# Two blocks of a transformer on one core: the memory's projections moved ahead of the mixing's output projection, one weight buffer for several stages, and attention maps started a chunk earlier

## The reference, cut to what matters

```python
for l in range(2):
    x = x + 0.5 * swiglu_ffn(rms_norm(x, ffn1_norm_g[l]), ...)        # ffn1
    proj = rms_norm(x, mix_norm_g[l]) @ w_mix_in[l]                   # mix_in
    y_rwkv = rwkv7_time_mix(...)      # 8 heads of 64; its end: y -> (y - mean) / sqrt(var + eps) * ln_g + ln_b + bonus, * g
    y_moba = moba_attention(...)
    x = x + concatenate([y_rwkv, y_moba]) @ w_mix_out[l]              # mix_out
    # memory_cross_attention, with 4 heads of 256:
    q    = rms_norm(x, xattn_norm_g[l]) @ w_q                         # xattn_q
    k, v = split(rms_norm(mem, mem_norm_g[l]) @ w_kv)                 # xattn_kv; mem: 256 x 1024
    x = x + (softmax(q @ k.T / 16) @ v) @ w_o                         # xattn_o
    x = x + 0.5 * swiglu_ffn(rms_norm(x, ffn2_norm_g[l]), ...)        # ffn2
# second block: proj = h @ w_in; mLSTM heads hm (4 x 128); differential attention hd (4 x 128)
merged = sigmoid(g_m) * (hm @ w_br_m) + sigmoid(g_d) * (hd @ w_br_d)
x = x + gate1 * (merged @ w_out)
x = x + gate2 * hierarchical_moe(...)
```

## Time and profile before

| | before |
|---|---|
| median of 3 runs | 2149.92 us (2147.03 to 2153.95) |
| the profiled execution: its time, its span | 2156.08 us, 2154.3 us |
| mean granted clock of TensorE | 0.963 |
| PE busy | 2025.2 us (94% of the span) |
| DVE busy | 1451.4 us (67%) |
| ACT busy | 1075.4 us (50%) |
| POOL busy | 328.7 us (15%) |
| moved by DMA | 401.93 MB, mean 187 GB/s |

### The profile page before, as it was taken

How to read it: one execution, slowest core, us unless ns; L and a number is a source line. 1 busy time by engine, 2 the same in 40 slices (tenths; PEclk the granted TensorE clock), 3 DMA queues, 4 the chain that set the end, 5 groups by cost and what they waited for, 6 DMA issues and landing times. The chain is left out here.

```text
span 2154.3 us, 34205 instructions
## 1 busy us (share of the span) xinstructions
PE 2025.2 (94%) x14008; PEld 1766.3 (82%) x14008; DVE 1451.4 (67%) x1876; ACT 1075.4 (50%) x1625; POOL 328.7 (15%) x182
## 2 busy tenths in 40 slices
PE   6999998699999989999987999998999889999999
PEld 5887887599888868879886997887899887888887
DVE  5774664475577467747637656764776557999997
ACT  5443662244544354437523445443655435777775
POOL 1650004000056006400040002630000000000000
PEclk9999999899999999999998999999999988999999
DMA  9653420054456456534203435653433324999995
GB/s 378 244 202 131 173 102 2 22 195 157 176 217 232 176 195 234 214 137 159 77 3 119 176 115 202 252 213 118 141 133 118 118 105 172 363 375 373 369 369 205
DMA packets 56854, 401.93 MB, mean 187 GB/s; under 512 B 6280, under 2 KB 7456, under 8 KB 8448
## 3 DMA queue, kind: packets, MB, share of 16 engines
q1 hardware_dynamic: 52320, 370.05, 46.1%
q0 software_dynamic: 4384, 29.74, 3.8%
HBM read 398.70 MB, written 1.06 MB: 186 GB/s over the span
## 5 line engine op out<-in xcount | busy, mean ns | idle before, releaser
L315 DVE TENSOR_TENSOR weights_lo<-ring,weights_hi 128x1024 fp32r<-128x1024 f32 x696 | 929.5, 1379 | 156.7 <-ACT weights_hi L305 155.8
L305 ACT CAST weights_hi<-ring 128x1024 fp32r<-128x1024 f32 x696 | 693.9, 1049 | 256.0 <-PE ps L329 255.7
L327 PE MATMUL ps<-weights_hi,act_hi 128*128 128x512 f32 (+1 forms) x832 | 320.3, 385 | 27.8 <-DVE weights_lo L315 23.3
L327 PE MATMUL ps<-act_hi,weights_hi 128*128 128x256 f32 x992 | 296.0, 298 | 26.4 <-DVE weights_lo L315 16.4
L329 PE MATMUL ps<-weights_hi,act_lo 128*128 128x512 f32 (+1 forms) x832 | 314.8, 378 | 0.0
L328 PE MATMUL ps<-weights_lo,act_hi 128*128 128x512 f32 (+1 forms) x832 | 313.8, 377 | 0.0
L328 PE MATMUL ps<-act_lo,weights_hi 128*128 128x256 f32 x992 | 288.1, 290 | 0.0
L329 PE MATMUL ps<-act_hi,weights_lo 128*128 128x256 f32 x992 | 287.6, 290 | 0.0
L327 PEld LDWEIGHTS ps<-act_hi,weights_hi 128*128 128x128 f32 x992 | 197.7, 199 | 34.6 <-DVE weights_lo L315 18.2
L327 PEld LDWEIGHTS ps<-weights_hi,act_hi 128*128 128x128 f32 x832 | 159.2, 191 | 57.6 <-DVE weights_lo L315 23.5
L328 PEld LDWEIGHTS ps<-act_lo,weights_hi 128*128 128x128 f32 x992 | 197.9, 200 | 0.1
(11 more groups left out here) (538 smaller groups left out, 3303.4 us busy)
## 6 DMA issues: line engine op xcount, KB each, us to landing
ring<-stream SPq DMA_DIRECT2D x348, 1024.0 KB, 4.9
stretch<-ada_in POOLq DMA_DIRECT2D x12, 1024.0 KB, 5.2
modulation_rows<-ada_in POOLq DMA_DIRECT2D x12, 1024.0 KB, 5.4
h<-mem_in POOLq DMA_DIRECT2D x2, 1024.0 KB, 5.3
consts<-w_consts SPq DMA_DIRECT2D x1, 1376.0 KB, 7.9
x<-x_in SPq DMA_DIRECT2D x1, 1024.0 KB, 4.9
stretch<-mem_in POOLq DMA_DIRECT2D x1, 1024.0 KB, 9.9
bias_slid<-bias_scratch SPq DMA_DIRECT2D x1, 1024.0 KB
```

The costliest lines, as they stand in the source:

```text
L305: core.nc.scalar.copy(self.hi[:, self.place(i), part], core.slot(chunk)[:, part]).then_inc(self.rounded.sem, 1)
L315: core.nc.vector.tensor_tensor(self.lo[:, self.place(i), part], core.slot(chunk)[:, part], self.hi[:, self.place(i), part].bitcast(F32), A ...
L327: nc.tensor.matmul(out, lhs[0], rhs[0], start=start, stop=False, **kw)
```

## The change

**In memory_stage** the stream's order is keys (chunks 0 to 3), values (4 to 7), mix_out (8 to 11), queries, output. The first products need no `y`: its centring, variance, norm, transposes and gating move out of `rwkv_stage` and stand between the products of chunks 0 to 4. Memory is normalized on POOL inside `rwkv_stage`, by four products of 128x1024. ACT copies keys and values. Chunk 0 is handed over by halves (`await_half`). x's norm before the queries becomes a `LateNorm` with its `add` and `total` at chunk 12; 1/rms enters as the scale of the scores. Buffers move to make room: `rwkv_g` lies in `b.decay`, `q`, `v`, `probs` in `b.stretch`.

**Splitters.** One runs from layer 0's xattn_kv over ffn2, layer 1's ffn1 and mix_in; ffn2 of layer 0 rounds two chunks further, and layer 1's ffn1 takes them with split=2.

**second_stage.** FIRST_TICK is 8, so that map 11's transposes and values fall within the chunk loop; the head norm of the attention stands earlier in the tail, each of its steps ahead of a branch product or of a chunk's split.

```diff
-        plan += [(("ffn1", layer), 3 * FFN_STEPS), (("mix_in", layer), 13), (("mix_out", layer), 4),
-                 (("xattn_kv", layer), 8), (("xattn_q", layer), 4), (("xattn_o", layer), 4),
+        plan += [(("ffn1", layer), 3 * FFN_STEPS), (("mix_in", layer), 13), (("xattn_kv", layer), 8),
+                 (("mix_out", layer), 4), (("xattn_q", layer), 4), (("xattn_o", layer), 4),
                  (("ffn2", layer), 3 * FFN_STEPS)]
...
-            for t in range(TT):
-                dve.wait_ge(y_done.sem, y_done.at(t + 1))
-                V(nc.vector.reduce_sum(stat[:, 0, 8 * t:8 * t + 8], bank8(t), AX))
-            V(nc.vector.tensor_scalar(stat[:, 0, :], stat[:, 0, :], 1.0 / 64, None, ALU.mult))
-            for t in range(TT):
-                V(tt(yt[:, t], bank8(t), stat[:, 0, 8 * t:8 * t + 8].unsqueeze(2).to_broadcast([P, 8, 64]), ALU.subtract))
-            V(tt(yq, yt, yt, ALU.mult))
...
-            nc.gpsimd.dma_start(h[:, :, :], b.mem_in).then_inc(b.mem_loaded.sem, 16)
+            nc.gpsimd.dma_start(h[:, :, :], b.mem_in).then_inc(mem_loaded.sem, 16)
+            pool.wait_ge(mem_loaded.sem, mem_loaded.at(16))
+            gain = core.param("mem_norm_g", layer)
+            for i in range(2):
+                part = h[:, 4 * i:4 * i + 4, :]
+                tt(part, part, b.mem_rs[:, :].unsqueeze(1).to_broadcast([P, 4, S]), ALU.mult).then_inc(mem_scaled.sem, 1)
+                pool.wait_ge(mem_scaled.sem, mem_scaled.at(i + 1))
+                tt(part, part, gain[:, 4 * i:4 * i + 4].unsqueeze(2).to_broadcast([P, 4, S]),
+                   ALU.mult).then_inc(b.mem_normed.sem, 1)
...
-            from_state(3, St[:, 1], 3).then_inc(y_done.sem, 1)
-            for t in range(TT):
-                pe.wait_ge(normed.sem, normed.at(t + 1))
...
+            from_state(3, St[:, 1], 3)
...
-                weights.await_split(pe, c)
+                if c:
+                    weights.await_split(pe, c)
                 if c >= banks:
                     sig, k = taken(c - banks)
                     pe.wait_ge(sig.sem, sig.at(k))
+                elif c >= 2:
+                    pe.wait_ge(centred.sem, centred.at(c - 1))
                 w = weights.parts(c, "p (k n) -> p k n", k=KB)
...
-                if c == 5:
-                    pe.wait_ge(added.sem, added.at(1))
-                    nc.tensor.matmul(ps[:, TURN, 0:S], core.const("ones"), rs[:, :], start=True,
-                                     stop=True).then_inc(summed.sem, 1)
-                elif c == values + 1:
+                if c == 3:
+                    for t in range(TT):
+                        pe.wait_ge(y_normed.sem, y_normed.at(t + 1))
+                        for i in range(4):
+                            ins = nc.tensor.transpose(ps[:, 4 + i, t * P:(t + 1) * P],
+                                                      yq[:, t, 2 * i:2 * i + 2, :].rearrange("p e n -> p (e n)"),
+                                                      core.const("ident"))
+                            if t == TT - 1:
+                                ins.then_inc(y_turned.sem, 1)
+                elif c == outs:
+                    acts.total(pe, TURN)
+                elif c == outs + 1:
...
+            weights.round_half(act, 0, 0)
+            round_mem(range(4))
+            weights.round_half(act, 0, 1)
+            round_mem(range(4, KB))
             weights.round(act, 1)
             weights.round(act, 2)
+            for t in range(TT):
+                act.wait_ge(centred.sem, centred.at(t + 1))
+                ins = nc.scalar.activation(yq[:, t], yt[:, t], ACT.Square)
+            ins.then_inc(y_squared.sem, 1)
             for c in range(queries):
+                if c < values:
                     act.wait_ge(core.used, start + c + 1)
                     nc.scalar.copy(place(c), bank(c)).then_inc(by_scalar.sem, 1)
+                elif c < outs:
+                    j = c - values
+                    act.wait_ge(by_vector.sem, by_vector.at(j + 1))
+                    acts.round(act, range(2 * j, 2 * j + 2))
+                    if j == 0:
+                        act.wait_ge(y_ready.sem, y_ready.at(KB))
+                    ins = nc.scalar.activation(y[:, 2 * j:2 * j + 2, :], x[:, 2 * j:2 * j + 2, :], ACT.Square)
+                    if c == outs - 1:
+                        ins.then_inc(acts.squared.sem, 1)
...
+            weights.subtract_half(dve, 0, 0)
+            split_mem(range(4))
+            weights.subtract_half(dve, 0, 1)
+            split_mem(range(4, KB))
             weights.subtract(dve, 1)
+            centre_y()
             weights.subtract(dve, 2)
...
             for c in range(queries):
...
-                if c < outs:
+                if values <= c < outs:
+                    j = c - values
                     dve.wait_ge(core.used, start + c + 1)
-                    dst = x[:, 2 * c:2 * c + 2, :]
+                    dst = x[:, 2 * j:2 * j + 2, :]
                     nc.vector.tensor_tensor(dst, dst, bank(c), ALU.add).then_inc(by_vector.sem, 1)
-                elif taken(c)[0] is by_vector:
+                    acts.subtract(dve, range(2 * j, 2 * j + 2))
+                elif c >= outs:
                     dve.wait_ge(core.used, start + c + 1)
                     nc.vector.tensor_copy(place(c), bank(c)).then_inc(by_vector.sem, 1)
+                if c == outs + 1:
+                    acts.invert(dve)
+                    V(nc.vector.tensor_scalar(row_scale[:, 0, :], rs[:, :], float(S) ** -0.5, None, ALU.mult))
+                    V(nc.vector.tensor_scalar(row_scale[:, 1, :], rs[:, :], -float(S) ** -0.5, None, ALU.mult))
                     front(0)
...
+                if c == 0:
+                    vary_y()
+                elif c == 1:
+                    norm_y()
                 if c + 1 < queries:
                     weights.subtract(dve, c + ways)
-                if c < 2:
-                    split_mem(range(4 * c, 4 * c + 4))
-                elif c == 4:
-                    dve.wait_ge(squared.sem, squared.at(1))
-                    nc.vector.reduce_sum(rs[:, :], h[:, :, :].rearrange("p k t -> p t k"), AX).then_inc(added.sem, 1)
+                if c == 4:
+                    gate_y()
+                elif c == 5:
+                    split_y(range(4))
                 elif c == 6:
+                    split_y(range(4, KB))
+                elif c == outs:
+                    acts.add(dve)
...
-    MAPS, M_MAPS, FIRST_TICK = 12, 4, 9
+    MAPS, M_MAPS, FIRST_TICK = 12, 4, 8
...
             branch_unit(BR_M, 0)
-            do_values(MAPS - 1)
-            branch_unit(BR_M, 1)
             pe.wait_ge(head_normed.sem, head_normed.at(4))
             head_sums(1, squares_d)
+            branch_unit(BR_M, 1)
+            head_turns(1)
             branch_unit(BR_M + 1, 0)
-            head_turns(1)
+            head_spreads(1)
             branch_unit(BR_M + 1, 1)
-            head_spreads(1)
             for c in range(BR_D, OUT):
                 branch_unit(c, 0)
...
             merge_m(0)
+            invert_heads(1)
             merge_m(1)
             weights.subtract(dve, BR_M + ways)
-            invert_heads(1)
             merge_m(2)
-            merge_m(3)
-            weights.subtract(dve, BR_M + 1 + ways)
             dve.wait_ge(head_spread.sem, head_spread.at(2))
             for j in range(4):
                 nc.vector.scalar_tensor_tensor(heads_d[:, j, :], heads_d[:, j, :], b.subln[:, 0:1],
                                                ps[:, E0 + j // 2, j % 2 * S:(j % 2 + 1) * S], ALU.mult,
                                                ALU.mult).then_inc(head_normed.sem, 1)
             split_y(1)
+            merge_m(3)
+            weights.subtract(dve, BR_M + 1 + ways)
             merge_d(0)
             merge_d(1)
             weights.subtract(dve, BR_D + ways)
...
-            move_turned(MAPS - 1)
-            take_values(MAPS - 1)
-            weights.round(act, BR_M + ways)
             root_heads(1)
             move_heads(1)
+            weights.round(act, BR_M + ways)
+            round_y(1)
             weights.round(act, BR_M + 1 + ways)
-            round_y(1)
             weights.round(act, BR_D + ways)
             round_merged(0)
...
+            run = ExitStack()
+            weights = Splitter(core, run, STREAM_AT["ffn1", 0][0], 3 * FFN_STEPS + 13)
             for layer in range(DEPTH):
...
-                        weights = Splitter(core, run, STREAM_AT["ffn1", layer][0], 3 * FFN_STEPS + 13)
...
-                    weights = Splitter(core, run, STREAM_AT["mix_out", layer][0], 20 + 3 * FFN_STEPS)
...
+                more = layer + 1 < DEPTH
+                ffn_stage(core, ("ffn1", layer), FFN_STEPS, weights, x, h, core.param("ffn1_norm_g", layer), h,
+                          modulation=(b, ada_in, y, 12 * layer, 6), loads=() if layer else loads[3:], split=2 if layer else 0,
+                          further=1, stretch=b.stretch)
```

(40 more changed lines are left out.)

224 lines of the change are left out of this document (99 added, 125 removed).

## The result

The changed kernel takes 2133.53 us (median of 4 runs, 2131.79 to 2137.32); before, the median over all runs beside it is 2151.7 us. The ratio over these runs is 0.9928, with a 95% interval of 0.9906 to 0.9949: 15.5 us faster by the ratio, between 11 and 20 us; the two medians alone are 18.2 us apart. The prediction was 2132, with 2118 to 2142 as its range.

A forecast was written before the change was run, and what follows sets the result against it. PE, busy 94% of the span, was taken as the bound, so its products plus its waits. Terms of 5.3 (layer 0), 5.0 (layer 1), 3.9 (Splitter) and 3.7 (second_stage) gave 17.9 us: 2149.92 to 2132, range 2118 to 2142.

The forecast's parts named there:

- the border: Between rwkv_stage and memory_stage: PE starts 13.5 us sooner, plus 0.5 for a shorter low-clock stretch; +14.0 per layer.
- the new wait behind chunk 12: In memory_stage PE's sum waits 7.2 us for DVE's reduction, plus tiny sums and low clock; -9.2 us per layer.
- the split weights at ffn1: One Splitter over the MLPs shortens PE's wait at layer 1's ffn1; gain 3.9 us, once.
- The second stage's term: In second_stage waits of 3.7 and 1.2 us go, one new wait of 1.2 comes; +3.7 us.
- the terms for the low clock: Slow PE clock after idles: 0.5 us gained at the border, 1.7 lost behind chunk 12, per layer.
- The transposes and what moved into the chunks: In memory_stage transposes return behind chunk 3, -1.0 us; y's norm work beside chunks 0 to 4 costs 0.
- Memory on POOL: At the border POOL's four products end 0.3 us after PE's last group in layer 1; nothing in layer 0.
- rival (b): POOL's chain, at 3.26 us per product, sets the border in both layers: 2136 to 2141 us; 12 in 100.
- Rival (c): POOL's products delay DVE's state additions at rwkv_stage's end, 4.7 us per layer: 2141.5 us; 5 in 100.
- (a): The wait behind chunk 12 does not come or is covered, 9.2 us more gain per layer: 2114 us; 4 in 100.
- (e): second_stage's reordering gives nothing, with four or five new waits of 1.2 us: 2136 us; 12 in 100.

The follow-up runs named there:

- e1: Changed kernel with PE's sums of squares moved from behind chunk 12 to behind chunk 13, ACT's root with them; 2119.24 us, ratio 0.987 to the kernel before.
- e2: Changed kernel with DVE's reduction of the squares ahead of chunk 15's subtraction; 2129.24 us, ratio 0.9903 to the kernel before.
- e9: Changed kernel with both DVE's reduction ahead of chunk 15's subtraction and PE's sums behind chunk 13; 2116.47 us, ratio 0.9861 to the kernel before.
- e5: Changed kernel with 56 extra products of 128x256 on PE behind chunk 12, filling the wait for the reduction; 2134.73 us, ratio 0.9945 to the kernel before.
- e7: Changed kernel with eight products of 128x1024 on POOL per layer in place of four; one execution, 2150.88 us.
- e11: Changed kernel unaltered, run again for a second profile and median; 2136.07 us, ratio 0.9926 to the kernel before, profiled execution 2144.19.
- e4: Changed kernel with a new Splitter at layer 1's ffn1, its first two chunks not rounded ahead, as before; 2139.84 us, ratio 0.9953 to the kernel before.
- e3: Changed kernel with the whole second stage as before (FIRST_TICK 9, the tail's old order); 2134.45 us, ratio 0.9925 to the kernel before.
- e10: Changed kernel with both the second stage as before and a new Splitter at layer 1's ffn1; 2141.81 us, ratio 0.9959 to the kernel before.
- e6: Changed kernel with the maps sooner (FIRST_TICK 8) but the tail's head norm in its old places; 2138.43 us, ratio 0.9961 to the kernel before.

## Why the prediction was right, and where its terms were off

The time lay inside the forecast's range, and the mechanisms that it named (the border, the new wait behind chunk 12, the split weights at ffn1) each stand in the profile at the size it gave. The second stage's term was too large, and the terms for the low clock were never separated from the spread between executions.

**The border (+14.0 forecast): right.** Forecast was PE's start 3.1 us behind its last group, measured 3.18 and 3.17; the shortening 13.5 against 13.4 twice. The half us for a shorter low stretch can't be told apart: the first 7.6 us ran at 0.78 in layer 0, and 7.8 us at 0.69 in layer 1, where before had 0.72 and 0.71.

**The transposes and what moved into the chunks (-1.0, 0): right within what is seen.** In chunks 0 to 11 no wait of PE stands in the profile, and the eight transposes take 1.04 us. The rest of memory_stage became 8.1 and 8.8 us longer, against 8.2 that the terms give without the border (-1.0, +1.5, -9.2, and +0.5 for the low clock).

**The wait behind chunk 12 (-9.2 per layer): right.** 7.2 forecast, 7.09 measured, in every profile of a version that keeps this order. The clock's part was forecast at 1.7; the 8.70 us behind the stops ran at 0.75 and 0.71, which is 2.2 and 2.5. e1, e2 and e9 show its cause and its price: DVE's order sets it (e2: 4.3), one chunk of cover removes most (e1: 1.5), both remove all (e9), 14 to 17 us from 14.2 us of idle. e5 leaves open how much of the rest is the low clock: filling the wait brought nothing.

**Memory on POOL (0.3 late in layer 1): wrong in its rule, small in size.** The prediction let the barrier wait for the end of POOL's last product. e7 shows that the next stage starts by that product's start, so it was 1.4 us early in both layers. The chain was as priced (1125.97 to 1134.57 in layer 1, 8.6 us for the four, with 8.7 forecast). In e11 POOL sets the border of layer 1, as rival (b) has it, but through a slower landing and not through dearer products: 1.0 us.

**Rival (c), POOL against DVE: refuted** for these instructions, by L1230's 0.42 in both layers.

**One Splitter (+3.9): right.** PE's wait at layer 1's ffn1 is 2.99 us in place of 6.90, and from ffn2's start to ffn1's it is 3.9 us less between the two profiles; e4 gives 6 with some 4 of uncertainty.

**second_stage (+3.7): the term that was mis-sized.** The prediction counted 4.9 of waits that go less one wait of 1.2. A third wait of 1.2, at L2581, is in the trace of before and was not among its rows; it changed too: in its place come four waits for `probs_T` (2.1 together; three with 1.3 in e11), and new are one of 0.45 and one of 1.0 for `mlstm_y_lo`. What is left is 2 to 3 us of idle (2.5 in the first profile). In time it can't be told from nothing: e3 is 0.9 above the changed kernel by the medians and 0.6 below by the ratios, e10 1.3 to 2.0 above e4. The 6.1 of the two profiles is 2.5 of waits and the rest clock; the second profile of before, with the same waits as the first, has 4.3 us less in this stage. e6 corrects the reason too: the forecast had both parts of the rearrangement remove the waits, and the long one goes by the norm's places alone.

**The total.** 17.9 forecast; with 2.5 for 3.7 and 0 for 0.3 it is 17.0. Measured are 15.5 (11 to 20) by the ratio, 15.9 (12 to 20) by e11's. The parts alone: memory 9 (5 to 13) with 10.3 forecast. The profiles' 22 is more because before's profiled execution lay 4 to 6 us above its median (2156.08), and the changed kernel's at its own.

The four pages separate the two causes. The time in which PE is not busy (span less PE's busy time) is 129.1 and 126.9 us in the two profiles of before, 110.5 and 110.8 in the two of the changed kernel: 16 to 19 us less, whichever are compared. PE's busy time, for the same products but four, is 2025.2 and 2017.3 before and 2021.5 and 2031.6 after: it moves by 8 and 10 us between two executions of one kernel, with the mean clock (0.963 and 0.967, 0.970 and 0.963). So the change's gain is in the waits, and most of what two executions of one kernel differ by goes with the clock. The forecast's terms for the clock (0.5 gained and 1.7 lost per layer) are smaller than that spread: that the total came out is no evidence for them, and as far as they helped it was luck. The forecast's 2138 for the profiled execution lies between the two that were taken, 2133.8 and 2144.2. The sum of the chances has a slip as well: below 2143.5 lie all of the forecast, (a), (b), (e) and most of (c), some 95 in 100, and not the 90 that it states.

## What to carry to other kernels

The waits at the border and behind chunk 12 were priced from rows to a tenth of a us (3.1 against 3.18, 7.2 against 7.09), since the chain behind each was read off instruction by instruction. In the second stage one of the three waits over 1 us was not listed, and the term came out too large. A wait that a move creates can be priced in the same way, and a move is not finished until the instruction that now waits has a full chunk of cover, as e9's moves gave it (14 to 17 us more than the change alone). A side engine with 1.4 us to spare at a barrier can become the path when a load lands late, as it did once here (e11). And the spans of one profile against one profile are worth little below 10 us here: each kernel's two profiled executions were 10 us apart with nearly the same waits. PE's idle time, which moved by 0.3 and 2.2 us between them, is the better thing to compare, and the ratio over many runs decides.

## What the runs showed of the hardware that was not expected

Behind a wait of 2.3 us the granted clock of TensorE was 1.00 in one execution and 0.68 or 0.69 in another for the next 3.7 us, in the same program at the same instruction (e11 and the first profile, above). At layer 1's ffn1, behind 2.99 us, it was 1.00 in both, and 0.56 in e9. Behind the stops of 7.1 us it was low in all seven profiles that have them. Low stretches of 3 to 7 us are in every profile at more than ten places, in the middle of stages too, and even behind a stretch in which PE never stood, as here in ffn2 of the changed kernel's first profile:

```profile
735.00:746.04 11.04, 11.04 (x64) 9.47 (x63) 6.06 (x7) 6.42 (x9) 0.00 (x0) 1.00 0.28 95
746.04:749.45 3.41, 3.41 (x10) 2.63 (x9) 2.50 (x3) 0.75 (x2) 0.00 (x0) 0.50 0.00 0
```

A mean clock of 0.963 against 0.970 went with an execution 10 us longer (e11 and the changed kernel's first). What chooses the places stays open.

Where POOL is the last to come to the barrier, the next stage's first instruction on ACT starts 0.2 us after POOL's last product starts (418.31 and 418.49, 1150.90 and 1151.07 in e7, 1142.03 and 1142.20 in e11), while that product is busy for 1.9 us in all. What needs the product's result must wait for its signal; the barrier does not stand for it.
